# Feed-forward weight sums of a bilinear pair: the first one made in place over the up block, the other three in one tile with two places for their parts

## The reference, cut to what matters

```python
hf = rms_norm_2(x, g_ffn[layer])
x = x + (jax.nn.silu(hf @ w_gate[layer]) * (hf @ w_up[layer])) @ w_down[layer]
...
return rms_norm_2(x, g_final)
```

## Time and profile before

| | us |
|---|---|
| median of 3 runs (2486.75 to 2487.12) | 2486.75 |
| the profiled execution | 2486.79 |
| its span | 2485.0 |
| PE busy | 2472.1 (99%) |
| DVE busy | 1771.4 (71%) |
| ACT busy | 1276.0 (51%) |

### The profile page before, as it was taken

One profiled execution on the slowest core, in us unless ns is written; L12 is line 12 of the kernel. 1 busy time (PEld: TensorE's weight loads), 2 busy tenths in 40 slices (PEclk: granted clock), 3 DMA queues, 4 the chain that ended last, 5 costly groups with the idle time before them and its releaser, 6 DMA issues.

```text
span 2485.0 us, 28892 instructions
## 1 busy us (share of the span) xinstructions
PE 2472.1 (99%) x10962; PEld 2036.7 (82%) x10962; DVE 1771.4 (71%) x2253; ACT 1276.0 (51%) x1619; POOL 192.0 (8%) x319
## 2 busy tenths in 40 slices
PE   9999999999999999999999999999999999999998
PEld 7888788888888888888888889888888888888887
DVE  6665665665675666675666866776678899988897
ACT  6454444444555444444545556566555555555554
POOL 0010000000011000010001100010100000000000
PEclk9999999999999999999999999999999999999999
DMA  9667666666688777776778754667766666666664
GB/s 333 208 223 221 208 212 211 204 218 202 210 241 259 231 233 223 226 234 210 228 238 262 235 180 149 233 203 220 229 211 220 220 217 212 210 211 218 218 210 148
DMA packets 263610, 545.31 MB, mean 219 GB/s; under 512 B 14768, under 2 KB 21040, under 8 KB 263088
## 3 DMA queue, kind: packets, MB, share of 16 engines
q1 hardware_dynamic: 242304, 477.39, 59.3%
q0 software_dynamic: 21168, 66.08, 9.5%
HBM read 508.29 MB, written 35.13 MB: 219 GB/s over the span
## 4 chain that ended last, share of the span: by engine, by line
PE 92%; DVE 5%; issue 2%; ACT 0%; DMA 0%; POOL 0%; DVEq 0%; ACTq 0%
PE job L2266 25%; PE job L2267 25%; PE job L2272 25%; DVE lo L2060 1%; PE group L2693 1%; PE group L2692 1%; PE group L2702 1%; PE att L2702 1%; PE att L2692 1%; PE att L2693 1%; PE job L2643 1%; PE job L2644 1%; PE job L2645 1%; DVE X L1343 1%; PE att L2643 1%
## 5 line engine op out<-in xcount | busy, mean ns | idle before, releaser
L1287 DVE TENSOR_TENSOR lo<-raw,hi 128x1024 fp32r<-128x1024 f32 (+1 forms) x736 | 879.2, 1213 | 504.8 <-ACT hi L729 483.9
L729 ACT ACTIVATE hi<-raw 128x1024 fp32r<-128x1024 f32 (+1 forms) x736 | 768.9, 1054 | 867.1 <-PE job L2272 808.9
L2266 PE MATMUL job<-hi,xh 128*128 128x512 f32 (+1 forms) x1696 | 663.0, 391 | 0.3 <-ACT hi L729 0.3
L2267 PE MATMUL job<-hi,xl 128*128 128x512 f32 (+1 forms) x1696 | 657.2, 388 | 0.0
L2272 PE MATMUL job<-lo,xh 128*128 128x512 f32 (+1 forms) x1696 | 451.0, 388 | 0.0
L2266 PEld LDWEIGHTS job<-hi,xh 128*128 128x128 f32 x1696 | 318.5, 188 | 68.5 <-issue 2.4
L2267 PEld LDWEIGHTS job<-hi,xl 128*128 128x128 f32 x1696 | 318.5, 188 | 66.4 <-issue 2.1
L2272 PEld LDWEIGHTS job<-lo,xh 128*128 128x128 f32 x1696 | 317.3, 188 | 65.1
L2266 PE MATMUL job<-hi,ah 128*128 128x512 f32 x832 | 325.9, 392 | 0.0
L2267 PE MATMUL job<-hi,al 128*128 128x512 f32 x832 | 323.8, 389 | 0.0
L2272 PE MATMUL job<-lo,ah 128*128 128x512 f32 x832 | 222.5, 389 | 0.0
(11 more groups left out here) (409 smaller groups left out, 2534.5 us busy)
## 6 DMA issues: line engine op xcount, KB each, us to landing
raw<-in_ret_w_in SPq DMA_DIRECT2D x94, 1024.0 KB, 5.2
raw<-in_pool_w_in SPq DMA_DIRECT2D x64, 1024.0 KB, 5.6
raw<-in_w_down SPq DMA_DIRECT2D x44, 1024.0 KB, 5.2
raw<-in_w_gate SPq DMA_DIRECT2D x72, 512.0 KB, 3.9
raw<-in_w_up SPq DMA_DIRECT2D x72, 512.0 KB, 4.8
raw<-in_ret_w_out SPq DMA_DIRECT2D x32, 1024.0 KB, 5.3
raw<-in_pool_w_out SPq DMA_DIRECT2D x32, 1024.0 KB, 5.3
raw<-in_w_in SPq DMA_DIRECT2D x28, 1024.0 KB, 6.0
```

Of the source, the lines that this page charges most:

```text
L729: act.activation(hi[:, (U.at * 2 + h) % HS, :, 0:n], src, ACT.Copy).then_inc(hi_ready, 1)
L1287: dve.tensor_tensor(lo[:, (U.at * 2 + h) % LS, :, 0:n], src, hi[:, (U.at * 2 + h) % HS, :, 0:n].bitcast(F32), ALU.subtract).then_inc(lo_re ...
L2266: pe.matmul(o, oh[:, kt, ts], w, start=first and k == 0, stop=False)
L2267: pe.matmul(o, ol[:, kt, ts], w, start=False, stop=False)
```

## The change

1. Sum 1 is written over the up block w[2] in `raw`, after sum 3 has been taken from it (`first_sums`: two instructions of 512 columns, sum 3 first). The up half then has 1024 columns for ACT and DVE, sum 1 and w[3], and ACT's `pair_high` waits for `sum1_made` in even units. Sum 1's product takes its parts from `hi` and `lo`.
2. The other three sums lie in one tile of 3 x 512 (`last_sums` makes sums 2 and 4). `high_sums` and `low_sums` handle all three in one instruction of 1536 columns, into the one or the other of two places in turn, so they wait for PE's use of the sums two even units back. `sums_used` is counted once a unit.
3. Places in the queues: ACT's `high_sums(i, v)` now stands whole at the end of unit v, behind its second high half and ahead of the next unit's first; DVE's `low_sums(i, v)` stands whole in unit v + 1, behind its first low half (and, in v = 1, behind `accumulate`). PE does the product of sum 1 right behind the wait for the second half, and waits once for all sums, after four products.
4. `gfb` lies over the parts of the sums. Its load moves from turn 0 to behind the last w_down load, with a wait for the last use of the sums.

```diff
-        sg, fg, gfb, fblk, fT, wsums, wsh, wsl, p1s, u2 = stage(
-            ("sg", [P, TT, NB]), ("fg", [P, TT, NB]), ("gfb", [P, D]),
-            ("fblk", [P, TT, 4, 4 * BK]), ("fT", [P, TT * 4, 4 * BK]),
-            ("wsums", [P, 4, NB]), ("wsh", [P, 4, NB], F32R), ("wsl", [P, 4, NB], F32R),
+        sg, fg, fblk, fT, wsums, wsh, wsl, p1s, u2 = stage(
+            ("sg", [P, TT, NB]), ("fg", [P, TT, NB]),
+            ("fblk", [P, TT, 4, 4 * BK]), ("fT", [P, TT * 4, 4 * BK]), ("wsums", [P, 3, NB]),
+            ("wsh", [P, 2, 3, NB], F32R), ("wsl", [P, 2, 3, NB], F32R),
             ("p1s", [P, NB]), ("u2", [P, NB]))
+        _, gfb = stage(("ffn_front", [P, 11 * NB]), ("gfb", [P, D]))
...
-                if u == 1:
-                    sp.wait_ge(half_used, 2 * FU)
-                    sp.dma_start(gfb[:, :], g_final.rearrange("(a n) -> a n", a=1).broadcast_to([P, D])).then_inc(gf_in, 16)
...
+            sp.wait_ge(sums_used, NBIL * (FC - PAIRED))
+            sp.dma_start(gfb[:, :], g_final.rearrange("(a n) -> a n", a=1).broadcast_to([P, D])).then_inc(gf_in, 16)
...
                     act.wait_ge(up_landed[U % RAW], up_count(i, v))
+                    if v in BILINEAR:
+                        act.wait_ge(sum1_made, sums_at(i, v) + 1)
                 act.wait_ge(half_used, U.value(2, h - HS + 1))
-                k = slice(1, 2) if h and v in BILINEAR else slice(0, 2)
-                act.activation(hi[:, (U.at * 2 + h) % HS, k, :], raw[:, U % RAW, h, k, :], ACT.Copy).then_inc(hi_ready, 1)
+                act.activation(hi[:, (U.at * 2 + h) % HS, :, :], raw[:, U % RAW, h, :, :], ACT.Copy).then_inc(hi_ready, 1)
...
+            def high_sums(i, v):
 
                 n = sums_at(i, v)
...
+                act.wait_ge(sum4_made, n + 1)
+                if n >= 2:
+                    act.wait_ge(sums_used, n - 1)
+                act.activation(wsh[:, n % 2, :, :], wsums[:, :, :], ACT.Copy).then_inc(sums_high, 1)
...
                     pair_high(U + v, i, v, 0)
-                    if v - 1 in BILINEAR:
-                        high_sums(i, v - 1, 1)
                     pair_high(U + v, i, v, 1)
                     if v in BILINEAR:
-                        high_sums(i, v, 0)
+                        high_sums(i, v)
...
+            def low_sums(i, v):
 
                 n = sums_at(i, v)
...
+                dve.wait_ge(sums_high, n + 1)
+                if n >= 2:
+                    dve.wait_ge(sums_used, n - 1)
+                dve.tensor_tensor(wsl[:, n % 2, :, :], wsums[:, :, :], wsh[:, n % 2, :, :].bitcast(F32), ALU.subtract).then_inc(sums_low, 1)
+
+            def first_sums(U, i, v):
...
                 if n:
-                    dve.wait_ge(sums_low, 2 * n)
-                dve.tensor_tensor(wsums[:, 0:2, :], w[:, 0:4:3, :], w[:, 2, :].unsqueeze(1).broadcast_to([P, 2, NB]),
-                                  ALU.add).then_inc(sums13_made, 1)
-
-            def sum_two(U, i, v):
+                    dve.wait_ge(sums_low, n)
+                dve.tensor_tensor(wsums[:, 0, :], w[:, 3, :], w[:, 2, :], ALU.add)
+                dve.tensor_tensor(w[:, 2, :], w[:, 0, :], w[:, 2, :], ALU.add).then_inc(sum1_made, 1)
+
+            def last_sums(U, i, v):
 
                 n, w = sums_at(i, v), four(U)
-                dve.wait_ge(sums13_made, n + 1)
-                dve.tensor_tensor(wsums[:, 2, :], wsums[:, 0, :], w[:, 3, :], ALU.add).then_inc(sum2_made, 1)
+                dve.wait_ge(sum1_made, n + 1)
+                dve.tensor_tensor(wsums[:, 1, :], w[:, 2, :], w[:, 3, :], ALU.add).then_inc(sum2_made, 1)
+                dve.wait_ge(sum2_made, n + 1)
+                dve.tensor_tensor(wsums[:, 2, :], wsums[:, 1, :], w[:, 1, :], ALU.add).then_inc(sum4_made, 1)
 
             def bilinear_low(U, i, v):
 
-                n, w = sums_at(i, v), four(U)
                 if v:
-                    early_sums(U, i, v)
+                    first_sums(U, i, v)
                 low_of(U, 0, slice(0, 2))
                 if v:
-                    sum_two(U, i, v)
-                low_sums(i, v, 0)
-                dve.wait_ge(sum2_made, n + 1)
-                dve.tensor_tensor(wsums[:, 3, :], wsums[:, 2, :], w[:, 1, :], ALU.add).then_inc(sum4_made, 1)
-                low_of(U, 1, slice(1, 2))
+                    last_sums(U, i, v)
+                low_of(U, 1, slice(0, 2))
...
                         if v - 1 in BILINEAR:
-                            low_sums(i, v - 1, 1)
+                            low_sums(i, v - 1)
                         low_of(U + v, 1, slice(0, 2))
...
                 wait_pair(U, 1)
+                product(BANK5[:, :], sh[:, s, 1], sl[:, s, 1], hi[:, b, 0], lo[:, b, 0], opens, closes)
                 product(BANK3[:, :], sh[:, s, 3], sl[:, s, 3], hi[:, b, 1], lo[:, b, 1], opens, closes).then_inc(half_used, 1)
-                pe.wait_ge(sums_low, 2 * n + 1)
-                product(BANK5[:, :], sh[:, s, 1], sl[:, s, 1], wsh[:, 0], wsl[:, 0], opens, closes)
+                pe.wait_ge(sums_low, n + 1)
                 if first:
                     wait_drained(pe, J - 1)
-                product(BANK7[:, :], sh[:, s, 0], sl[:, s, 0], wsh[:, 1], wsl[:, 1], first, last).then_inc(sums_used, 1)
-                pe.wait_ge(sums_low, 2 * n + 2)
-                ins = product(BANK6[:, :], sh[:, s, 2], sl[:, s, 2], wsh[:, 2], wsl[:, 2], first, last)
+                product(BANK7[:, :], sh[:, s, 0], sl[:, s, 0], wsh[:, z, 0], wsl[:, z, 0], first, last)
+                ins = product(BANK6[:, :], sh[:, s, 2], sl[:, s, 2], wsh[:, z, 1], wsl[:, z, 1], first, last)
...
-                product(BANK4[:, :], xh[:, k + 1, two], xl[:, k + 1, two], wsh[:, 3], wsl[:, 3], opens, closes).then_inc(sums_used, 1)
+                product(BANK4[:, :], xh[:, k + 1, two], xl[:, k + 1, two], wsh[:, z, 2], wsl[:, z, 2], opens, closes).then_inc(sums_used, 1)
```

More of the change, by code:

```diff
@@ L316, in build @@
         up_landed = [sem(f"up_landed{n}") for n in range(RAW)]
-        sums13_made, sum2_made, sum4_made = sem("sums13_made"), sem("sum2_made"), sem("sum4_made")
+        sum1_made, sum2_made, sum4_made = sem("sum1_made"), sem("sum2_made"), sem("sum4_made")
         sums_high, sums_low, sums_used = sem("sums_high"), sem("sums_low"), sem("sums_used")
@@ L1179, in pair_high @@
                     act.wait_ge(up_landed[U % RAW], up_count(i, v))
+                    if v in BILINEAR:
+                        act.wait_ge(sum1_made, sums_at(i, v) + 1)
                 act.wait_ge(half_used, U.value(2, h - HS + 1))
-                k = slice(1, 2) if h and v in BILINEAR else slice(0, 2)
-                act.activation(hi[:, (U.at * 2 + h) % HS, k, :], raw[:, U % RAW, h, k, :], ACT.Copy).then_inc(hi_ready, 1)
-            def high_sums(i, v, part):
+                act.activation(hi[:, (U.at * 2 + h) % HS, :, :], raw[:, U % RAW, h, :, :], ACT.Copy).then_inc(hi_ready, 1)
+            def high_sums(i, v):
                 n = sums_at(i, v)
[L1187 to L1194, removed]
+                act.wait_ge(sum4_made, n + 1)
+                if n >= 2:
+                    act.wait_ge(sums_used, n - 1)
+                act.activation(wsh[:, n % 2, :, :], wsums[:, :, :], ACT.Copy).then_inc(sums_high, 1)
             drain(Pos(FJ), Pos(FU + 7), lambda t: sg[:, t, :], RS, ACT.Silu)
@@ L2061, in low_of @@
                                   hi[:, (U.at * 2 + h) % HS, k, :].bitcast(F32), ALU.subtract).then_inc(lo_ready, 1)
-            def low_sums(i, v, part):
+            def low_sums(i, v):
                 n = sums_at(i, v)
[L2066 to L2072, removed]
+                dve.wait_ge(sums_high, n + 1)
[3 more added lines that the diff above has]
+            def first_sums(U, i, v):
                 n, w = sums_at(i, v), four(U)
@@ L2120, in start_next @@
                 if i < FC and 0 in BILINEAR:
-                    early_sums(U, i, 0)
-                    sum_two(U, i, 0)
+                    first_sums(U, i, 0)
+                    last_sums(U, i, 0)
             def second_turn():
@@ L2157, in ffn_turn @@
                     if v in BILINEAR:
+                        if v - 1 in BILINEAR:
+                            low_sums(i, v - 1)
                         bilinear_low(U + v, i, v)
@@ L2658, in bilinear_unit @@
                 a, b = (U.at * 2) % HS, (U.at * 2 + 1) % HS
+                z = n % 2
                 wait_pair(U, 0)
```

## The result

The changed kernel takes **2518.68 us** (median of 4 runs, 2518.40 to 2519.23) against 2486.75: a ratio of 1.0128 with an interval of [1.0111, 1.0146]. It is slower by 31.9 us; the forecast was 2517.0 in a range of 2508 to 2530. The profiled execution took 2518.95, its span is 2517.2.

The account below looks back on a forecast made before the run. PE, busy 99%, was taken to bound the kernel, with DVE nearly bounding it at turn heads. Turns 3 to 10 (27.8) and turn 2 (1.55), together 29.3, plus load 0.5 gave 29.8 on 2486.79: 2517 us, range 2508 to 2530.

Parts of the forecast that it names:

- Prices: Durations from the trace: 1536 columns 1.67 us start to start on DVE, 1.40 on ACT; PE's restart 0.22.
- v = 0: Unit 0 of a turn: accumulation, then low sums, make PE 0.65 us late, in nine turns.
- v = 2: Unit 2: hidden work on DVE and ACT's wait for the last sums make PE 2.6 us late, eight turns.
- v = 4: Unit 4: the DVE and ACT round takes 10.21 us against PE's 10.30, so no stall.
- v = 6: Unit 6: ACT's hidden_high (0.97) before the next high half makes PE 0.9 us late, nine turns.
- The old stall: PE's 0.68 us stall in unit 2 of the kernel before, turns 3 to 10, was to go.
- The moved load: Final gains' load behind the last weights, sharing DMA engines with the last turned block: 0.5 us, bounds nothing to 2.1.
- Rival 1: Next high half is made early enough in the turns, so only the old 5.4 us goes: 2481 us, chance 0.05.
- Rival 2: ACT's wait is covered, without DVE's 1.5 us idle: unit 2 1.1 late, unit 6 not: 2497 us, chance 0.08.
- Rival 3: Clock drops after each of eight pauses of 2.6 us, 1.5 us each: 2522 to 2529 us, chance 0.10.

Follow-up runs that it names:

- e3: Changed kernel with DVE's low_sums(v) moved to the end of its own unit v, behind its second low half: 2488.12 us.
- e2: Changed kernel with hidden_high and hidden_low, the splits of the hidden product, moved from unit v = 6 to v = 7: 2515.37 us.
- e4: Kernel before the change, with only the load of the final gains moved behind the last w_down load: 2486.75 us.
- e1: Changed kernel with ACT's high_sums(v) moved behind the first high half of unit v + 1: 2494.74 us.
- e7: Kernel before the change, with 0 to 6 and then 2 filler DVE additions, by turns, delaying the low half in v = 2: 2510.19 us.
- e10: Kernel before the change, with 2 and 3 filler DVE additions in alternate turns delaying the low half in v = 2: 2504.35 us.
- e8: Changed kernel with DVE's hidden product moved from unit v = 1 to v = 3: 2517.33 us.
- e9: Changed kernel with one place for the parts of the sums instead of two: 2518.30 us.
- e11: Kernel before the change, with the products of the sums reading a fixed tile instead of the sums' parts, their values left out: 2484.55 us.

## Why the prediction was right

**What bounds the kernel** was read rightly: PE waits on DVE's sums and halves, and time moved only there. Equal work and a new order was the right frame; e3 shows it best, which differs from the kernel after only in where DVE's low sums stand and is 30.6 us faster.

**Prices.** 1.67 start to start and 1.75 to the end for the 1536 columns on DVE: measured 2153.13 − 2151.46 = 1.67, and 1.75. On ACT 1.40: measured 2162.07 − 2160.68 = 1.39. PE's start after a low sum's end: 0.06 to the start and 0.10 on the matmul, 0.16 instead of 0.22.

**v = 0.** 0.65 forecast, 0.60 measured, nine times; the whole difference is that start of PE.

**v = 2.** 2.6 forecast, 2.55 measured, eight times. The step that decided it held to a few hundredths, from the turn's first matmul: high sums at 10.64 (measured 2160.68 − 2150.06 = 10.62), the next low half at 13.15 (13.09), the end of the low sums at 16.03 (15.98). DVE's idle "about 1.5" was 1.37.

**v = 4.** No pause, as forecast.

**v = 6: the step that failed.** "0.9 late, nine turns" came true in three. The size was right where it occurred, 0.85 to 0.95, and e2 shows that the two splits of the hidden product were its cause. The prediction's chain had the 0.97 of ACT's `hidden_high` in it; the rows of v = 6 have DVE's `hidden_low` there, with 1.14, while ACT's next high half is made beside it. The two are near each other, so the size came out by luck. And in the six turns in which the clock had fallen, PE lost 1.5 us that the other engines didn't, and the 0.9 was covered.

**The old stall** of 0.68 is gone eight times, and turn 2 is longer by 64.35 − 62.96 = 1.39 where 1.55 was forecast.

**The moved load** was priced at 0.5 us; e4 shows nothing.

**Rivals.** Rival 1 (faster) fell at the point it named: the low sums in v = 0 end too late. Rival 2 (ACT's wait is covered) described e1 well (2497 against 2494.74), but not the kernel after: v = 2 is then 1.1 late, v = 6 not at all. Rival 3 (the clock drops), with 0.10, came true on top of the forecast's own pauses. The prediction had named a fall of the clock as a sign that it was wrong, and by that sign it was wrong here, though its time held. Its sum had the low clock at nothing because the pauses were short beside those of 4.3 us and more at the end; 9.2 us were lost to it, and e7 and e10 show that a pause of this size is long enough in the kernel before as well. The rival's own time, 2522 to 2529, was too high, in part because it had the clock fall in every turn and not in six of eight. Its price of 1.5 was near the 1.54 measured, but that was luck: the 3.0 us behind it are the length of a window that was asked for at the end of the span, in which PE did nothing, and not that of a low stretch behind a pause.

The Trainium skill ("TensorE: Matmul & The Clock Gate", Why this matters for your kernels) advises against idle gaps between bursts of matmuls because they bring the half clock back. It means longer gaps than the 2.28 us of this kernel. In the runs, three of three from 3.20 us up brought it back, as it says, but 27 of 37 between 2.16 and 2.47 us did so too, and the measurement decides.

**The sum by turns**, measured: six with the low clock of about 67.6 (3.96 more than 63.64), two of 66.98 (3.34 more) and turn 2 (1.39 more) make 23.8 + 6.7 + 1.4 = 31.9 us, of a span longer by 32.2. The forecast had 29.3. It was close by luck, because two errors partly cancelled: 9.2 us of low clock not counted, and some 5.4 us of pauses in v = 6 (0.9 in six turns) counted that were covered.

## What to carry to other kernels

Before moving a step in an in-order queue, walk through what stands behind its wait: here ACT's idle 1.35 us at the sums returned as DVE's idle 1.37 and lay on PE's path, and one call moved back (e1) or the consumer moved ahead of the dependent half (e3) took it away. Merging small operations in larger ones makes the first of them as late as the last. Where TensorE will pause for 2.2 us or more, count the slow matmuls behind the pause as well, and let what it costs cover the small pauses that follow it.

## What the hardware showed that was not expected

- **Pauses of 2.2 to 2.5 us can halve the clock, and don't always.** Idle time of 2.16 to 2.47 us before a matmul was followed by the 1.2 GHz level in 6 of 8 turns in each of the kernel after, e2, e8 and e9, and in three of five in e7 and e10: 27 of 37 in all. Idle time of 1.74 to 1.76 was followed by it in none of six, and the 0.83 of e1 in none of eight. The low stretch was about 3.4 us long, some eight matmuls at 0.427 us, and 13 of them behind the 4.64 us in e7. It can begin well after PE has resumed: in the kernel after at 2100.01, with PE running again since 2098.49. What decides between like pauses wasn't found out.
- **Matmuls that read the sums' parts are 3% slower.** Where the moving operand is one of these parts, matmuls start 0.233 us apart and not 0.227, and some ordinary ones behind them too; with a fixed tile in its place they start 0.227 apart (e11). Why stays open.
- **One wide instruction costs no more than its columns.** The 1536-column form costs 1.67 us on DVE and 1.39 on ACT, one step of 512 columns over the 1024 form in each case (1.13 and 0.97), as had been estimated.
